# A fused HGRN2 and SwiGLU layer: regrouped down products, weight sums on VectorE, another order of seven products

## What is computed

```python
def _swiglu(x, w_gu, w_down):
    gate, up = jnp.split(x @ w_gu, 2, axis=-1)
    return (jax.nn.silu(gate) * up) @ w_down

def _hgrn2(h, layer, state, w_in, lower_bounds, out_gain, w_out):
    q, f, i, g = jnp.split(h @ w_in, [nk, 2 * nk, 2 * nk + HG_HEADS * HG_DV], axis=-1)
    ...                                     # chunkwise recurrence over 64 frames
    o = _rmsnorm(o.transpose(0, 2, 1, 3), out_gain).reshape(B, T, HG_HEADS * HG_DV)
    return (o * jax.nn.silu(g.astype(F32))).astype(h.dtype) @ w_out, state

x = x + mix
x = x + _swiglu(_rmsnorm(x, norm_ffn[layer]), ffn_w_gu[layer], ffn_w_down[layer])
```

## Time and profile before

| | us |
|---|---|
| median of 3 runs | 2914.08 |
| lowest and highest | 2912.82, 2914.98 |
| profiled execution, whole | 2920.44 |
| profiled execution, span of the trace | 2918.7 |
| TensorE busy in the span | 2680.2 |
| VectorE / ScalarE / GpSimd busy | 1809.4 / 1254.4 / 390.4 |

### The profile page before, as it was taken

One profiled execution on the slowest core, in us unless ns is written; L12 is line 12 of the kernel. 1 busy time (PEld: TensorE's weight loads), 2 busy tenths in 40 slices (PEclk: granted clock), 3 DMA queues, 4 the chain that ended last, 5 costly groups with the idle time before them and its releaser, 6 DMA issues.

```text
span 2918.7 us, 53924 instructions
## 1 busy us (share of the span) xinstructions
PE 2680.2 (92%) x16804; PEld 2426.4 (83%) x16804; DVE 1809.4 (62%) x3132; ACT 1254.4 (43%) x2287; POOL 390.4 (13%) x285
## 2 busy tenths in 40 slices
PE   8999889999879998999969997999987998899994
PEld 8999889989868876998948886989876887799893
DVE  6666776666556657666645766756554665766663
ACT  5555343333345544433325554434334554443342
POOL 3111242332111111000011111000001111100001
PEclk9999999999999998999989998999998999899997
DMA  5222244444432223655533222647443222466553
GB/s 172 93 61 83 93 164 144 166 165 145 141 118 69 76 72 128 211 172 170 177 102 94 76 68 87 205 143 238 141 133 109 72 72 87 131 197 181 164 167 115
DMA packets 203398, 379.57 MB, mean 130 GB/s; under 512 B 23168, under 2 KB 23200, under 8 KB 203056
## 3 DMA queue, kind: packets, MB, share of 16 engines
q1 hardware_dynamic: 202896, 369.73, 40.8%
q0 software_dynamic: 384, 8.44, 0.8%
HBM read 331.67 MB, written 52.74 MB: 132 GB/s over the span
## 4 chain that ended last, share of the span: by engine, by line
PE 73%; DMA 8%; DVE 7%; issue 5%; ACT 3%; SPq 2%; POOL 2%; DVEq 0%; ACTq 0%; POOLq 0%
PE ps L421 14%; PE ps L423 13%; PE ps L422 13%; PE ps L511 7%; PE ps L513 7%; PE ps L512 7%; DMA w_raw<-w_all 5%; DMA kept_sum<-g_x 2%; DMA g_raw<-w_all 1%; PE ps_s L511 1%; PE ps_u L331 1%; PE ps_s L513 1%; PE ps_s L512 1%; PE ps_s L310 1%; DVE g_lo L1063 1%
## 5 line engine op out<-in xcount | busy, mean ns | idle before, releaser
L511 PE MATMUL ps<-h,g_hi 128*128 128x256 f32 (+1 forms) x2112 | 620.1, 294 | 49.8 <-DVE ebuf L1103 32.0
L877 DVE TENSOR_TENSOR w_lo<-w_raw,w_hi 128x512 fp32r<-128x512 f32 x512 | 367.2, 723 | 417.8 <-ACT w_hi L714 417.5
L513 PE MATMUL ps<-h,g_lo 128*128 128x256 f32 (+1 forms) x2112 | 607.6, 288 | 0.0
L512 PE MATMUL ps<-h,g_hi 128*128 128x256 f32 (+1 forms) x2112 | 606.2, 287 | 0.0
L421 PE MATMUL ps<-a_hi,w_hi 128*128 128x512 f32 (+1 forms) x1200 | 451.5, 376 | 124.6 <-DVE fbuf L1137 63.1
L714 ACT ACTIVATE w_hi<-w_raw 128x512 fp32r<-128x512 f32 x512 | 316.0, 624 | 508.6 <-PE ps L423 269.6
L421 PE MATMUL ps<-h_hi,w_hi 128*128 128x512 f32 (+1 forms) x1280 | 476.1, 372 | 36.2 <-DVE fbuf L1137 24.2
L511 PEld LDWEIGHTS ps<-h,g_hi 128*128 128x128 f32 x2112 | 404.6, 192 | 66.0 <-DVE ebuf L1103 36.4
L423 PE MATMUL ps<-h_hi,w_lo 128*128 128x512 f32 (+1 forms) x1280 | 458.0, 358 | 0.0
L422 PE MATMUL ps<-h_lo,w_hi 128*128 128x512 f32 (+1 forms) x1280 | 456.8, 357 | 0.0
L422 PE MATMUL ps<-a_lo,w_hi 128*128 128x512 f32 (+1 forms) x1200 | 443.3, 369 | 0.0
(11 more groups left out here) (160 smaller groups left out, 3932.7 us busy)
## 6 DMA issues: line engine op xcount, KB each, us to landing
w_raw<-w_all SPq DMA_DIRECT2D x516, 256.0 KB, 2.6
g_raw<-w_all SPq DMA_DIRECT2D x286, 256.0 KB, 3.2
g_x<-kept_sum SPq DMA_DIRECT2D x132, 256.0 KB, 3.3
g_hi<-kept_hi SPq DMA_DIRECT2D x132, 256.0 KB, 2.9
g_lo<-kept_lo SPq DMA_DIRECT2D x132, 256.0 KB, 3.4
...
```

The costliest lines, as they stand in the source:

```text
L511: pe.matmul(out, g_hi[:, o, k, :].bitcast(F32R), hh, start=(k == 0 and not more), stop=False, skip_group_check=True)
L512: pe.matmul(out, g_hi[:, o, k, :].bitcast(F32R), hl, start=False, stop=False, skip_group_check=True)
L513: mm = pe.matmul(out, g_lo[:, o, k, :].bitcast(F32R), hh, start=False, stop=last, skip_group_check=True)
L877: nc.vector.tensor_tensor(w_lo[:, r, :, :], w_raw[:, r, :, :], w_hi[:, r, :, :].bitcast(F32), ALU.subtract).then_inc(w_lo_ready, 1)
```

## The change

It has these parts.

- **Groups.** `GROUPS` becomes 6, 8 and 8 feature tiles instead of 8, 8 and 6; the first group takes the last six features of w_gu and w_down (`GU_FROM`, `DN_FROM`).
- **Order of the seven products.** A11, S2, S3, S1, A22, A12, S4 instead of A11, S2, A22, S1, S3, A12, S4; S3 and A22 trade banks. VectorE's and ScalarE's splits follow that order. In the first feature tile of a block all five first products run over three quarters of the depth before the last quarter, where A11 alone did so over all of it.
- **Weight sums** of block 0 move from GpSimd to VectorE (`weight_sum`).
- **SyncE.** w_out pieces 6 and 7 are queued ahead of the gate/up loads of feature tile 0; in blocks 1 to 3 those loads go in three parts between the following pieces. In block 0's gate/up loop the loads of A21 and A11 go ahead of the S3 store, A22 behind it, A12 last.
- **y** has a buffer of its own, `y_out`, four tiles over `g_raw` and part of `g_x`; the wait for its store moves from the eviction to the add, and next-block tiles are taken two behind instead of one.
- **Norm weight** on ScalarE: `h2_high` scales from `xres`, VectorE's L1039 goes; VectorE makes T1 and the first low part between the two tiles of a pair.
- **Down** starts without waiting for the last product's bank (blocks 1 to 3: nor for the others). The second norm is taken on ScalarE at the end of feature tile 0 instead of the start of tile 1. `a_hi` starts at a multiple of 128 bytes.

```diff
-GROUPS = ((0, 8), (8, 8), (16, 6))
+GROUPS = ((0, 6), (6, 8), (14, 8))
+GU_FROM, DN_FROM = (16, -6, -6), (4, 0, 2)
-A11, S2, A22, S1, S3, A12, S4 = range(OPERANDS)
-H_OF = (0, 4, 6, 3, 5, 1, 2)
+A11, S2, S3, S1, A22, A12, S4 = range(OPERANDS)
+H_OF = (0, 4, 5, 3, 6, 1, 2)
+    y_out, y_out_end = place("y_out", [P, 4, T0], offset=g_at)
-    bank_of = (bank_a, bank_b, bank_e, bank_d, bank_c, bank_a, bank_d)
+    bank_of = (bank_a, bank_b, bank_c, bank_d, bank_e, bank_a, bank_d)
...
                         if s == 0:
                             pe.wait_ge(g_copied, 2 * J)
-                        pe.wait_ge(g_added, 4 * J)
+                            if first(b):
+                                pe.wait_ge(g_added, 4 * J - 2)
+                        else:
+                            pe.wait_ge(g_added, 4 * J if first(b) else 4 * J - 1)
...
+                def scaled(s):
+                    m = TILE_AT[done + s]
+                    act.wait_ge(x1_ready, KT * b + done + s + 3)
...
+                    nc.scalar.activation(out, two(xres[:, m, 0:T], T), ACT.Copy, scale=gffn[:, m:m + 1]).then_inc(h2_scaled, 1)
...
+            def weight_sum(j, o):
+                if o == S1:
+                    dve.wait_ge(g_loaded[RAW_A21], 16 * (j + 1))
+                    dve.wait_ge(g_loaded[RAW_A22], 16 * (j + 1))
+                    wait(dve, g_lo_ready, OPERANDS * j)
+                    nc.vector.tensor_tensor(g_x[:, 0], g_raw[:, RAW_A21], g_raw[:, RAW_A22], ALU.add).then_inc(g_sum_ready, 1)
+                elif o == S2:
+                    dve.wait_ge(g_loaded[RAW_A11], 16 * (j + 1))
+                    dve.wait_ge(g_sum_ready, 4 * j + 1)
+                    wait(dve, g_sum_stored[1], 16 * j)
+                    nc.vector.tensor_tensor(g_x[:, 1], g_x[:, 0], g_raw[:, RAW_A11], ALU.subtract).then_inc(g_sum_ready, 1)
...
                     if m < len(ahead):
-                        gu_low(b, GROUPS[f + 1][0], ahead[m])
-                    if last and m > 0:
-                        residual_tile(m - 1, TB, b + 1, gmix)
+                        j1 = GROUPS[f + 1][0]
+                        if first(b) and m == 0:
+                            for o in (S1, S2, S3):
+                                weight_sum(j1, o)
+                        if first(b) and m == A12:
+                            weight_sum(j1, S4)
+                        gu_low(b, j1, ahead[m])
+                    if last and m > 1:
+                        residual_tile(m - 2, TB, b + 1, gmix)
...
-                        if last:
-                            dve.wait_ge(y_stored[s], 16 * ((KT // 2) * b + m // 2) + 1)
...
-                    nc.vector.tensor_tensor((fbuf[:, s, 0:T] if last else xres[:, m, 0:T]), fbuf[:, s, 0:T], xres[:, m, 0:T],
+                    if last and m >= 4:
+                        dve.wait_ge(y_stored[s], 16 * ((KT // 2) * b + m // 2 - 1) + 1)
+                    nc.vector.tensor_tensor((y_out[:, m % 4, 0:T] if last else xres[:, m, 0:T]), fbuf[:, s, 0:T], xres[:, m, 0:T],
...
-                load_pair(b, 0)
-                load_pieces(b, OUT0 + RING + 2, DN0 + RING)
+                load_pieces(b, OUT0 + RING + 2, OUT0 + 2 * RING)
+                if first(b):
+                    load_pair(b, 0, 0)
+                    load_pieces(b, OUT0 + 2 * RING, DN0 + RING)
+                else:
+                    sp.wait_ge(y_lo_ready, HEADS * (b + 1))
+                    for part in range(3):
+                        load_kept(b, 0, 0, part)
+                        q = OUT0 + (2 + part) * RING
+                        load_pieces(b, q, q + RING)
```

More of the change, by code:

```diff
@@ L538, in gate_up @@
                     bank_free(J, o)
-                    if after_down is not None and o in (A11, A22):
+                    if after_down is not None and o in (A11, S1):
                         pe.wait_ge(dn_done, after_down + (1 if o == A11 else 2))
@@ L699, in head @@
                         wait(act, ke_ready, G)
+                        if not (recur or first(b)):
+                            for s in range(2):
+                                act.wait_ge(y_stored[s], 16 * (KT // 2) * b + 1)
                         nc.scalar.activation(e_neg[:, 0:T], grel[:, 0:T], ACT.Exp, scale=-1.0).then_inc(e_ready, 1)
@@ L786, in gate_up @@
                 nc.scalar.activation(fbuf[:, 1, 0:n], bank_a[:, 0:n], ACT.Copy).then_inc(g_copied, 1)
[L787 to L789 removed]
+                if norm_at is not None:
+                    norm(b, T, norm_at)
+                high(A12, S4)
             def next_tile(b, m, i, s):
@@ L1086, in gate_up, with low, total @@
                     a_product(b, T, j - 1)
-                for o in nxt:
-                    if o <= S2:
-                        gu_low(b, j + 1, o)
+                def low(*operands):
+                    for o in operands:
+                        if o in nxt:
+                            gu_low(b, j + 1, o)
+                def total(*operands):
+                    for o in operands:
+                        if first(b) and more:
+                            weight_sum(j + 1, o)
+                low(A11)
+                total(S1, S2)
                 dve.wait_ge(g_done, OPERANDS * J + S2 + 1)
```

293 lines of the change are left out of this document (145 added, 148 removed).

## The result

| | before | after |
|---|---|---|
| median of 4 runs, us | 2914.5 | 2835.6 |
| lowest and highest | 2912.8, 2917.0 | 2834.8, 2838.7 |
| ratio, 95% interval | | 0.9731, 0.9714 to 0.9747 |
| span of the profiled execution | 2918.7 | 2834.3 |
| mean granted clock of TensorE | 0.961 | 0.972 |

The account below looks back on a forecast made before the run. The kernel was taken as TensorE-bound wherever TensorE isn't waiting, so a change pays only at its waits. Terms -40.6 - 39 - 7 - 8 + 3 = -91.6 took 2914.1 to 2822 us, range 2797 to 2852.

Parts of the forecast that it names:

- groups: Down groups, all blocks: the first group's tiles get shorter, the last group's cost as before; -40.6 us, ends -30 and -46.
- w_out pieces, blocks 1 to 3: w_out stage: pieces 6 and 7 queued ahead of nine transfers let VectorE start 8.1 us earlier a block.
- products over three quarters of the depth: First gate/up tile: 36 matmuls, 4.3 us a block, no longer stand behind the last h2 tile.
- block 0: w_out stage to the first a_lo: Block 0's w_out stage: a 5.10 us wait goes, products ahead give 3, weight sums cost; -7 us, ends -2 and -12.
- block 0: loop: Block 0's gate/up: the loop through S4's store stays, 14.0 us a tile, 0.2 more, over 17 tiles; +3, ends -3 and +10.
- down start, all blocks: Start of down: TensorE no longer waits for the last product's bank; -8 us, ends -2 and -9.
- The ring: Last down group: add, SyncE's issues, piece load, split, eviction and add fix 9.35 us a tile, with room for 24 matmuls.
- The second rival, the half clock: Last down group: TensorE's clock stays low, a 24-matmul tile takes 10.1 us, 24 us more in all: 2846; chance 0.06.
- The third, short tiles held at 5.62: First down group: VectorE or the loads hold tiles at 5.62 us, so the 40.6 go: 2863; chance 0.05.
- The w_out stage: Blocks 1 to 3: earlier start, products ahead and some of the half-clock stretch; 13 us a block, -39, ends 8 and 16.
- The term for the start of a_hi: The 128-byte start of a_hi: worth nothing, since no row shows a dependence.
- the microsecond at a_lo: Block 0's gate/up: VectorE regains 1.0 us a tile without GpSimd's sums, but the loop leaves it no place.

Follow-up runs that it names:

- groups_back: The changed kernel with groups of 8, 8 and 6 feature tiles in the old order of features: 2876.3 us, 40.6 more than the changed kernel.
- pieces_behind: The changed kernel with w_out pieces 6, 7 and later queued behind the nine transfers of gate/up tile 0 again: 2859.4 us, 23.8 more.
- a11_whole: The changed kernel, but in a block's first feature tile A11 runs over the whole depth at once, the other four over three quarters: 2835.9 us.
- gpsimd_sums: The changed kernel with block 0's four weight sums back on GpSimd: 2832.4 us, 3.2 less.
- pair_early: The changed kernel; block 0 stores S2's pair before loading A21 and A11, S4 before S1's pair, and ScalarE awaits only the overwritten pair's store: 2807.5 us.
- all_three: The changed kernel plus pair_early, last-down-group pieces issued ahead of the add, and the first tile's A22 split ahead of the norm-factor wait: 2710.4 us.
- all_gpsimd: all_three with block 0's four weight sums on GpSimd: 2708.9 us.

## Why the prediction was right, and where not

| term, us | forecast | measured | by |
|---|---|---|---|
| groups | -40.6 | -40.6 | groups_back |
| w_out pieces, blocks 1 to 3 | -24 (8.1 each) | -20 | pieces_behind |
| products over three quarters of the depth | up to -13 (4.3 each) | 0 | a11_whole |
| down and gate/up matmuls, blocks 1 to 3 | 0 | some -15 | rows of the two traces |
| block 0: w_out stage to the first a_lo | -7 | -0.5 (-5.0 at the norm's factor) | rows of the two traces, below |
| block 0: loop | +3 | +11 | a_lo of both traces |
| down start, all blocks | -8 | some -8 | last a_lo to first eviction, before and groups_back; no run of its own |

The measured column adds up to -73; what is left of the 84.4 is in the main some 3 us a block of the w_out stage that no run takes apart (below). The down start is read from two traces whose groups are alike: with 24 matmuls the first eviction comes 4.80 us after the last a_lo before and 3.91 in groups_back (0.2 of it are the shorter matmuls), with 18 matmuls 3.39 and 2.57; in block 0 5.32 and 4.94, 3.72 and 2.79.

**The ring** was read rightly in the earlier trace rows, and its fixed price is why the term came true: 9.32 and 9.38 with 18 and 24 matmuls, the first group at 4.05 (4.2 was forecast), block 0's at 4.5 (4.8). That it is right to the tenth is luck: block 0 gave 12.9 and not 11.2, the others 7.8, 9.7 and 9.4 and not 9.8 each. The second rival, the half clock, didn't come: in the last group the granted clock is 0.88 in the mean, 0.84 before. The third, short tiles held at 5.62, fell by the rows of the first group.

**The w_out stage** came to about the forecast by parts that differ from it. The start was worth 6.6 instead of 8.1. The step on the products ahead failed: it took the 36 matmuls as a chain that ends the stage, while the same paragraph had said that VectorE sets the stage. Had I held to that, the 4.3 would have been nothing. The stage is still some 11 us shorter in block 2: from the norm's first matmul of the last head to the first down eviction it took 149.83 us before and 117.07 now, 32.8 less, of which two feature tiles are 20 and the shorter first down product is 1.4. The start is 7.3 of this 11 in block 2, the down start and six shorter gate/up tiles are 0.7 each. Some 3 have no run: the norm weight on ScalarE and the new places of the splits weren't tried alone.

**Matmuls.** The term for the start of a_hi was set at nothing "since no row shows a dependence", and so it wasn't looked for. In block 2 the two down groups outside the ring give 1.3 us each, and gate/up 0.11 x 22 = 2.4 (10.08 before, 9.97 after): 5 a block. The down part is the alignment, as the kernel without it shows; the gate/up part is not (9.88 without it), and what else in the change brings it wasn't tried. This unforecast gain covers the w_out term's 4.3: that the later blocks look rightly forecast is luck.

**Block 0's loop** is the larger part of the miss. The mechanism was right, and the rows show it turn by turn, but the sum took 14.0 from a working of 14.4, and 14.67 was measured. On VectorE's side, S2 sum to the end of A22's split, 7.7 was forecast and 532.88 + 0.68 - 525.43 = 8.1 measured, in most turns: the half-wide eviction L1151 (0.45) stands inside the loop and wasn't counted. On SyncE's side, from there to the next S2 sum, 6.7 was worked out and 6.6 is the mean (6.87 in the turn shown); taking another 0.4 off for "two transfers fewer in the queue" was wrong. The parts of the 6.7 were off against each other: the five issues take 2.6 and not 3.1, the landing of S4's store takes 3.7 in the mean (4.10 in the turn shown) and not 3.39. Issues follow one another 0.5 us apart and landings 0.7: in the turn shown A22's load and the five stores, issued from 533.74 to 536.31, land at 536.74, 537.39, 538.23, 538.90, 539.78 and 540.41. So what faster issuing saves, the queue takes back. The S3 store is hardly in this queue: in the turn shown it landed at 533.71, just ahead of A22's load, in the other turns of the loop at most 0.5 us behind its issue. 14.67 - 13.85 = 0.8 in thirteen turns are 10.6; each group's last looped tile is 1.2 shorter than before, and the first tile of the second and the third group 1.8 and 2.2 longer.

**Block 0's w_out stage** was 3.9 us ahead at the last residual add (359.21 against 363.15), 6.3 at the eviction of the banks of S1 and A22 in tile 0 (L1163 at 374.11, L1103 at 380.41 before), 5.0 at the product with the norm's factor, and only 0.5 at the first a_lo. The pieces brought 5.2 (pieces_behind, block 0). The four weight sums on VectorE cost 3.1 of it at the last residual add, which comes at 356.12 in gpsimd_sums; the prediction had set them against GpSimd's interference. TensorE and VectorE in the changed kernel, then VectorE in the kernel before:

```profile
374.11 0.75 DVE L1163 TENSOR_TENSOR ebuf<-ps,ebuf 128x576 f32<-128x576 f32 x1
374.96 0.58 PE L518 MATMUL ps<-h,g_hi 128*128 128x288 f32 x1 [5.77 <-DVE g_lo L1114]
381.78 0.76 DVE L1168 TENSOR_TENSOR ebuf<-ebuf,xrstd 128x576 f32<-128x576 f32 x1 [6.92 <-ACT xrstd L603]
390.96 0.69 DVE L1102 TENSOR_TENSOR g_x<-g_x,g_raw 128x512 f32<-128x512 f32 x1 [1.80 <-DMA kept_sum<-g_x]
392.95 0.75 DVE L1127 TENSOR_TENSOR a_lo<-fbuf,a_hi 128x576 fp32r<-128x576 f32 x1
```
```profile
386.79 0.76 DVE L1111 TENSOR_TENSOR ebuf<-ebuf,xrstd 128x576 f32<-128x576 f32 x1 [5.02 <-ACT xrstd L593]
393.46 1.76 DVE L1078 TENSOR_TENSOR a_lo<-fbuf,a_hi 128x576 fp32r<-128x576 f32 x1
```

From the factor to the first a_lo it takes 11.17 us now and took 6.67 before: that is where the 4.5 us go. The first a_lo now stands behind the S2 sum of tile 2, and that sum waits for the S4 store of tile 1 (issued at 386.08, landed at 390.83). It is the store loop again, half a turn ahead of where the forecast began to count it. In pair_early, with the stores out of the way, a_lo comes at 391.01, 1.9 earlier; the rest is the row itself, which now holds three sums (S4, S1, S2). The forecast costed the moved work for the steady loop and not for its start.

The 5.77 us of TensorE is no split. TensorE has done tile 0's first six products and goes on with S4 at 374.96, 0.1 after the end of L1163 (374.11 + 0.75 = 374.86; in all_three 374.54 and 374.64). S4 shares its bank with S1, and L1163 empties it; the split that the profile names had ended by 374.19. The sums S1, S2 and S3 of tile 1 stand ahead of that eviction, but they aren't where time is lost: in all_gpsimd, without them, the wait is 6.63, and from the last residual add to this eviction it takes 15.7 us against 14.9 in all_three.

**GpSimd's sums.** The prediction said that the microsecond at a_lo would find no place. gpsimd_sums and all_gpsimd bear that out with the loop closed and with it open: -3.2 and -1.4 us with the sums on GpSimd. The shared port of the Trainium skill (SBUF — State Buffer, "SBUF: two separate sides") is visible in each trace, as 1.77 at a_lo before and as 2.01 for two splits in gpsimd_sums; it costs VectorE about 0.7 to 1 us a tile, and the four sums cost VectorE 4 x 0.6 (0.61 from the start of one to the next instruction). Under 4 us in either pair, the two kernels can't be told apart.
